# Who issues the stores of the split weights: GpSimd in place of SyncE, in a two-layer hybrid encoder kernel

## What is computed

```python
h = rmsnorm(x, pre_norm)
proj = jnp.einsum('bld,de->ble', h, w_in.astype(F32))      # 1024 x (6656 + 24) per layer
...                                                        # conv, SiLU, the three mixers, gates
mixed = jnp.concatenate([o_a, o_b, o_c], axis=-1)
out = jnp.einsum('ble,ed->bld', mixed, w_out.astype(F32))
return x + rmsnorm(out, post_norm).astype(x.dtype)
```

## Time and profile before

| | |
|---|---|
| Median of 3 runs | 2197.93 us (2197.86 to 2205.15) |
| The profiled execution | 2202.74 us, its span 2200.9 us |
| TensorE busy | 2136.7 us, 97% |
| VectorE, ScalarE, GpSimd busy | 1359.7, 887.1, 489.9 us |
| Mean granted clock of TensorE | 0.988 |
| DMA | 410.88 MB, 187 GB/s on average |

### The profile page before, as it was taken

The page is one execution under the profiler, slowest core; times in us unless marked ns, Lnnn a source line. Parts: engine busy times, 40 slices in busy tenths (PEclk is TensorE's granted clock), DMA queues, the critical chain, the costliest instruction groups (busy, mean ns, idle before and its releaser), DMA issues. The chain is left out here.

```text
span 2200.9 us, 39104 instructions
## 1 busy us (share of the span) xinstructions
PE 2136.7 (97%) x15396; PEld 1973.4 (90%) x15396; DVE 1359.7 (62%) x2692; ACT 887.1 (40%) x1779; POOL 489.9 (22%) x432
## 2 busy tenths in 40 slices
PE   7999999999999999999999999999999999999996
PEld 6888988999898899899989798889988989899996
DVE  5777667445677765523567777673547777745334
ACT  5545377233433355211354444753324343643111
POOL 3444333231000021100333343423300000201001
PEclk9999999999999999999999899999999999999998
DMA  6646356676533265444564744566665233753434
GB/s 240 236 173 230 124 192 220 230 273 227 209 125 121 102 228 201 154 165 161 193 238 154 287 147 163 185 216 257 242 231 190 87 134 126 253 170 140 167 116 163
DMA packets 98197, 410.88 MB, mean 187 GB/s; under 512 B 11168, under 2 KB 12256, under 8 KB 84192
## 3 DMA queue, kind: packets, MB, share of 16 engines
q1 hardware_dynamic: 97440, 407.98, 53.0%
q10 hardware_dynamic: 576, 0.41, 0.1%
HBM read 257.18 MB, written 151.16 MB: 186 GB/s over the span
## 5 line engine op out<-in xcount | busy, mean ns | idle before, releaser
L1172 PE MATMUL ps<-w_hi,hT_hi 128*128 128x256 f32 x1792 | 524.6, 293 | 1.7 <-DVE hT_lo L1491 1.7
L1172 PE MATMUL ps<-w_low,hT_hi 128*128 128x256 f32 x1792 | 506.0, 282 | 0.0
L1172 PE MATMUL ps<-w_hi,hT_lo 128*128 128x256 f32 x1792 | 502.9, 281 | 0.0
L2165 POOL TENSOR_TENSOR w_low<-w_loaded,w_hi 128x512 fp32r<-128x512 f32 x208 | 288.5, 1406 | 452.9 <-ACT w_hi L1893 452.9
L1172 PEld LDWEIGHTS ps<-wk 128*128 128x128 f32 x2336 | 307.9, 192 | 56.7 <-issue 18.1
L1172 PE MATMUL ps<-wk 128*128 128x128 f32 (+2 forms) x2336 | 343.2, 283 | 12.9 <-issue 5.1
L1172 PEld LDWEIGHTS ps<-w_hi,hT_hi 128*128 128x128 f32 x1792 | 339.6, 189 | 4.4 <-DVE hT_lo L1491 2.3
L1172 PEld LDWEIGHTS ps<-w_low,hT_hi 128*128 128x128 f32 x1792 | 339.2, 189 | 2.2 <-issue 1.9
L1172 PEld LDWEIGHTS ps<-w_hi,hT_lo 128*128 128x128 f32 x1792 | 339.5, 189 | 0.0
L1172 PE MATMUL ps<-hT_hi,w_hi 128*128 128x512 f32 x768 | 328.6, 428 | 2.1 <-POOL w_low L2165 2.0
L1172 PE MATMUL ps<-hT_lo,w_hi 128*128 128x512 f32 x768 | 302.9, 394 | 0.0
(11 more groups left out here) (197 smaller groups left out, 3219.9 us busy)
## 6 DMA issues: line engine op xcount, KB each, us to landing
w_loaded<-in_w_in SPq DMA_DIRECT2D x104, 512.0 KB, 5.1
w_split<-w_hi SPq DMA_DIRECT2D x52, 1024.0 KB, 7.5
w_split<-w_low SPq DMA_DIRECT2D x52, 1024.0 KB, 9.5
w_hi<-w_split SPq DMA_DIRECT2D x104, 512.0 KB, 6.0
w_low<-w_split SPq DMA_DIRECT2D x104, 512.0 KB, 7.2
wo_loaded<-in_w_out SPq DMA_DIRECT2D x32, 512.0 KB, 4.3
wk<-cum_rows SPq DMA_DIRECT2D x32, 512.0 KB, 4.6
wo_split<-wo_hi SPq DMA_DIRECT2D x32, 512.0 KB, 7.0
```

The lines of the kernel that those rows point to most:

```text
L1172: return nc.tensor.matmul(o, a, b, start=start, stop=stop)
L2165: tt(w_lo[at], wr[at], w_hi[at], ALU.subtract)\
```

## The change

The entries `keep` go out of SyncE's list. GpSimd issues the two stores of a piece itself, right behind its fourth subtraction: first the high part, then, after waiting for its own subtractions, the low part. Semaphores and transfers are the same.

```diff
@@ in the list of loads
             loads.append((where[release] if n >= W_RING else -5 if n == 0 else -2, n, ("in", p, i)))
-            if p % 2 == 0:
-                loads.append((where["proj", p, i, 0, Q - 1], n, ("keep", p, i)))
@@ in SyncE's program
-                elif kind == "keep":
-                    sp.wait_ge(S["w_lo_ready"], 4 * split_no(n) + 4)
-                    sp.dma_start(w_split[key[2], 0], w_hi[:, n % W_RING, :].bitcast(F32)).then_inc(w_kept[n % W_RING], 16)
-                    sp.dma_start(w_split[key[2], 1], w_lo[:, n % W_RING, :].bitcast(F32)).then_inc(w_kept[n % W_RING], 16)
@@ in GpSimd's program, step "split"
                     tt(w_lo[at], wr[at], w_hi[at], ALU.subtract)\
                         .then_inc(S["w_lo_ready"], 1)
+                    if j == 3:
+                        pool.dma_start(w_split[s[2], 0], w_hi[:, n % W_RING, :].bitcast(F32)).then_inc(w_kept[n % W_RING], 16)
+                        pool.wait_ge(S["w_lo_ready"], 4 * split_no(n) + 4)
+                        pool.dma_start(w_split[s[2], 1], w_lo[:, n % W_RING, :].bitcast(F32)).then_inc(w_kept[n % W_RING], 16)
```

## The result

| | before | after |
|---|---|---|
| median | 2199.59 us (2197.86 to 2205.15, 9 runs) | 2207.99 us (2206.59 to 2212.20, 9 runs) |
| ratio to before | | 1.0037 (95% interval 1.0028 to 1.0046) |
| the profiled execution | 2202.74 us, span 2200.9 | 2206.59 us, span 2204.8 |
| mean granted clock | 0.988 | 0.988 |

The change costs 0.37%, 8.1 us (the medians alone are 8.4 us apart): within the half per cent that the prediction called no change, but clearly not zero. The two profiled executions differ by 3.9 us only, so their traces account for about half of it; the rest rests on medians.

A forecast was written before the change was run, and what follows sets the result against it. TensorE, busy 97% of the span, was taken as the bound. Terms -1.0 + 3.0 + 1.0 = +3.0 us on the 2197.9 median gave 2201 us; forecast's own range 2195 to 2209, overall range 2186 to 2220.

The forecast's parts named there:

- The sum with high prices: All terms at their high prices, plus 1.7 us of clock for each of two stalls: +13 us.
- Late loads, -1 us: Nine raw-weight loads, 40 us late together behind SyncE's stores, leave earlier; TensorE gains 1 us, bounds 0 to 3.6.
- Hold of GpSimd, 2.1 us: Per piece, GpSimd is held by two store issues of 1.0 us and 0.1 us waiting for its own subtraction.
- D*x at 320 and 1404, 3 us: GpSimd's D*x product, delayed behind the stores, holds VectorE's mask and stalls TensorE about 1.5 us at each place.
- The load of piece 61, 1 us: Load issued at 1223.06, without slack, runs beside piece 60's stores and lands 0 to 5 us later; costs 1 us.
- Most with slack: Of 22 loads issued within 8 us after stores begin, most land in 5.1 us, before ScalarE reads them.
- "nothing" rival: SyncE's stalls were harmless and GpSimd's time is idle time: 2198 us, chance 0.10.
- A long hold: GpSimd held 5 us or more per piece, decisive from about 4 us: 2223 to 2261 us, chance 0.10.
- the port case: VectorE and GpSimd hinder each other, each store issue stretched by 1.0 us, hold 4.1 us: 2210 us, chance 0.12.
- The other long case: GpSimd's second store issue waits until the first store has left; within the slower rival of chance 0.10.
- SyncE's wait at L1101 under 60 us: Sign: SyncE's wait for stores to land, ahead of loads, falls from 343 us to under 60 in all.

The follow-up runs named there:

- sp_early_three: Kernel before, all stores still SyncE's, but those of pieces 18, 54 and 70 placed early, behind the split of their last quarter: 2211.22 us, ratio 1.0044.
- pool_hold4: Kernel before, stores unchanged, with four chained power operations on GpSimd behind each piece's last subtraction: 2216.48 us, ratio 1.0077.
- after_18_old_b: Changed kernel with the stores of pieces 18 and 70 back with SyncE at their old place: 2202.41 us, ratio 1.0003.
- after_18_54: Changed kernel with the stores of pieces 18, 54 and 70 back with SyncE at their old place: 2199.27 us, ratio 0.9995.
- only_54: Kernel before, with GpSimd issuing the stores of piece 54 alone, early: 2207.48 us, ratio 1.0030.
- late_only: Kernel before, with GpSimd issuing only the stores of nine pieces that stood ahead of late loads (2, 3, 22, 54, 55, 59, 60, 61, 74): 2207.72 us, ratio 1.0033.
- only_18: Kernel before, with GpSimd issuing only the stores of pieces 18 and 70, early: 2204.49 us, ratio 1.0023.

## Why the prediction came out as it did

No change beyond half a per cent was forecast and found, and 2208 lies within both ranges. But the 8 us are not the 3 us of the sum: two of its terms came out near nothing, and the largest one is missing. That the time still fell inside is in part luck: losses of some 12 us that the prediction did not name were nearly offset by gains that it did not name either. (The sum with high prices, +13 from 2197.9, gives 2211, while the forecast's own range ends at 2209.)

- **Late loads, -1 us: the loads as said, the gain not seen.** Counted by the same rule, loads over 1 us late went from 9 with some 40 us to 3 with some 15 us (61, 62 and 63, which stand behind stores of x). Piece 4's goes at 57.89, forecast 57.6. TensorE's stall at 71.4 is 1.84 us (1.85 in the earlier trace rows). The changed kernel is 1.6 us ahead at 76, because its clock stays at 1.00 behind that same stall (0.53 before); by 300 it is level. sp_early_three, which moves no store so early, is as far ahead at 77, so this is not the loads' doing. A gain of up to 1 us is neither shown nor excluded.
- **Hold of GpSimd, 2.1 us: it is 1.14.** The step taken wrongly is that software descriptors cost more like a GpSimd instruction than like SyncE's issue; the lower bound, 1.0, was near. The figure of about 1 us that the Trainium skill (DMA: Bandwidth & Descriptors, Latency and other measured facts) gives is to the first byte and is no measure of how long the engine is held: 0.61 and 0.53 us here.
- **D*x at 320 and 1404, 3 us: nothing.** VectorE's wait behind it rose from 8.5 to 10.6 us in all, and TensorE shows no stall there. The chain was right (pool_hold4), the term mis-sized: held 1.1 us it is absorbed.
- **The load of piece 61, 1 us: about right.** It went out at 1231.1 behind stores of x, landed in 6.6 us (6.3 before), and TensorE lost 1.2 us at 1232 to 1235 (waits behind `w_low` 3.8 us in all, 2.0 before).
- **Missing: the stores against everything else in flight.** "Most with slack" was said of the 22 loads near the stores, and it looked only at ScalarE's use of those loads. It did not ask which other transfer, behind them in the same engines, is late: the stores of a unit of output weights (2 places, 0.23%), and the load of such a unit, which had no slack (1 place, 0.30% by itself). The three together, with nothing else changed, give 0.44% and explain the 0.37%.
- **Missing on the other side: the stall at 1620.** SyncE's last pair of stores stood just ahead of a load of x. It is one of the things that the other 49 pairs changed; they are worth -0.05% together (-0.14 to +0.03), so the "nothing" rival has their sum right, though not each place: 1620 gains and 1138 loses.
- **Rivals.** A long hold needs 4 us, as the prediction said; pool_hold4 at 4.4 us costs 17 us. GpSimd's issues never exceed 772 ns with VectorE busy 62% of the span, so the port case did not occur. The Trainium skill (SBUF — State Buffer, SBUF: two separate sides) would have them stand still while VectorE runs in a two-port mode. No row shows in which mode VectorE ran; the longest issue here is 0.16 us over the median. The other long case, a second issue that waits for the first store, did not occur in the 52 pairs of the change, but it did in four of the runs beside it (last section).
- **What was to show it.** "SyncE's wait at L1101 under 60 us" was wrong: it is 224.3 (L1099 now), while its wait for TensorE in the same entry rose from 193.1 to 337.0 us. With fewer entries to serve SyncE comes sooner to the next load and stands there, which costs nothing.

Open: how the loss divides. Piece 54 costs 0.30% alone, but between after_18_old_b and after_18_54 only 0.08 points, and 18 and 70 cost 0.23% alone, 0.34 as a difference. The parts need not add, because each move changes what the next transfer meets: in after_18_54 the stall at 1112 goes and one of 2.20 us comes at 1138, and the 3 us at 1620 stand in only_54 and sp_early_three but not in the change, after_18_old_b or after_18_54. How the DMA engines share their time among queues, no row shows; what is shown is the time to landing.

## What to carry to other kernels

When a transfer is made free to leave earlier, list what is in flight at its new time, in all queues: not only the load that waits for it, but those that it pushes back. Here 25 us less of late loads gave TensorE nothing that can be seen, because none of them was what it waited for, and 2 MB a few us ahead of a transfer that was wanted cost it 2 us and more each time. The load to fear for is the one that lands just as it is used: it shows no wait in the trace of before. Where one of many such moves collides, leave that one at its old place: 49 of 52 moved without loss. And where the profile names "issue" for a wait, look at what the sequencer's own wait instruction waits for and when that landed, before another cause is sought.

## What the runs showed of the hardware

- A 1 MB store issued by GpSimd holds it 0.53 to 0.77 us; the same from SyncE has a median of 0.43.
- In eight pairs (after_18_54 three, late_only and after_18_old_b two each, only_18 one) GpSimd stood 4.1 to 8.2 us between its two issues, and issued the second 0.35 or 0.36 us after the first store had landed: in after_18_54 at 1130.38, landed at 1130.02. Each of the eight is GpSimd's first pair behind one or more that were SyncE's. In the 52 pairs of the change it never happened. Why it happens where it does is open.
- With 2 MB of stores just issued, SyncE's issue of the next two 512 KB loads takes 1.60 us together (0.81 before), whoever issued the stores: 1.61 in sp_early_three.
- The 512 KB load of `wo_hi` near 1112, issued within 6 us behind 2 MB of stores, took 7.5 to 8.9 us to land, and 4.7 to 5.3 at the same place without them, again whoever issued the stores.
- A stall of 3.13 us took TensorE's granted clock with it: 0.69 over 1112 to 1120, with 1.00 before. In after_18_54 a stall of 2.20 us at 1138 did not: the clock was 1.00 over the 8 us behind it.
